# Layer 2 of a two-layer hybrid block: convolved tiles 2 to 5 and retention keys as three channel pairs of seven quarter products

## The reference, cut to what matters

```python
hx = modulate(rms_norm(x, norm1_g[layer]), mx[0], mx[1])
hc = modulate(rms_norm(ctx, norm1_g[layer]), mc[0], mc[1])
oc, ox = token_mixers(hc @ w_in[layer], hx @ w_in[layer], ...)
...
# gated delta net: q, k, v are convolved over the tokens of each half
qkv = jax.nn.silu(depthwise_conv_centred(qkv, conv_w))     # 5 taps per channel
# retention: latent queries and keys are turned by their position
ql, kl = apply_rope(ql, cos, sin), apply_rope(kl, cos, sin)
```

## Time and profile before

| | us |
|---|---|
| median of 3 runs | 2078.41 (2075.3 to 2080.1) |
| profiled execution, its own time | 2080.07 |
| its span (first to last instruction) | 2078.1 |
| PE busy | 1959.0 (94%) |
| DVE busy | 732.0 (35%) |
| ACT busy | 351.4 (17%) |
| POOL busy | 301.8 (15%) |

### The profile page before, as it was taken

The page is one execution under the profiler, slowest core; times in us unless marked ns, Lnnn a source line. Parts: engine busy times, 40 slices in busy tenths (PEclk is TensorE's granted clock), DMA queues, the critical chain, the costliest instruction groups (busy, mean ns, idle before and its releaser), DMA issues.

```text
span 2078.1 us, 53833 instructions
## 1 busy us (share of the span) xinstructions
PE 1959.0 (94%) x24244; PEld 1393.3 (67%) x24244; DVE 732.0 (35%) x1625; ACT 351.4 (17%) x845; POOL 301.8 (15%) x264
## 2 busy tenths in 40 slices
PE   6999987899999999999879899899999999999996
PEld 4885557578888888885677666466655666666664
DVE  5586547346553555356575500100101010000102
ACT  3005535121000000213552300000000000000001
POOL 0872524000000000096360000000000000000000
PEclk9999999999999999999989899899999999999998
DMA  9224562422213222321202999999999999999996
GB/s 348 83 82 162 203 243 84 163 82 80 83 61 102 82 82 76 128 82 41 82 3 104 350 366 378 403 408 342 328 404 401 403 401 398 401 405 399 408 392 235
DMA packets 181552, 481.99 MB, mean 232 GB/s; under 512 B 11738, under 2 KB 48458, under 8 KB 181194
## 3 DMA queue, kind: packets, MB, share of 16 engines
q1 hardware_dynamic: 177008, 473.99, 60.8%
q0 software_dynamic: 768, 2.62, 0.4%
q10 hardware_dynamic: 3546, 1.91, 0.3%
HBM read 476.39 MB, written 2.10 MB: 230 GB/s over the span
## 4 chain that ended last, share of the span: by engine, by line
PE 80%; DVE 6%; DMA 5%; POOL 3%; issue 3%; SPq 2%; ACT 1%; DVEq 0%; ACTq 0%; POOLq 0%
PE bank L785 77%; PE bank L788 3%; DMA ring<-in_moe_w_dram 3%; POOL ring L3562 2%; DMA ring<-in_w_in_dram 1%; POOL work L3564 1%; DMA ring<-in_ada_w_dram 1%; SPq L738 1%; DVE small L2695 1%; SPq L748 1%; ACT ring L1889 1%; DVE tmpB L2568 1%; DVE ring L2861 0%; POOL work L3560 0%; DVE ring L2523 0%
## 5 line engine op out<-in xcount | busy, mean ns | idle before, releaser
L785 PE MATMUL bank<-ring,hT 128*32 128x256 f32 (+1 forms) x10112 | 591.9, 380 | 6.0 <-DMA ring<-in_moe_w_dram 5.4
L785 PEld LDWEIGHTS bank<-ring,hT 128*32 128x32 f32 (+1 forms) x10112 | 357.5, 112 | 227.6 <-issue 19.6
L785 PE MATMUL bank<-ring 64*64 64x64 f32 (+5 forms) x4184 | 429.3, 292 | 30.0 <-issue 9.1
L785 PEld LDWEIGHTS bank<-ring 64*64 64x64 f32 (+3 forms) x4184 | 356.2, 157 | 89.6 <-issue 38.9
L785 PE MATMUL bank<-hT,ring 128*128 128x256 f32 (+1 forms) x1448 | 363.2, 407 | 6.3 <-DMA ring<-in_w_in_dram 2.6
L785 PEld LDWEIGHTS bank<-hT,ring 128*128 128x128 f32 x1448 | 278.2, 194 | 75.9 <-issue 35.5
L785 PE MATMUL bank<-ring,gates 128*32 128x256 f32 x4928 | 276.8, 382 | 9.2 <-DMA ring<-in_moe_w_dram 8.8
L785 PEld LDWEIGHTS bank<-ring,gates 128*32 128x32 f32 x4928 | 158.8, 111 | 119.4 <-DMA ring<-in_moe_w_dram 14.0
L1889 ACT ACTIVATE gates<-bank 128x256 f32<-128x256 f32 (+2 forms) x139 | 58.3, 465 | 902.1 <-PE bank L788 517.4
L3484 DVE TENSOR_TENSOR gates<-gates,bank 128x512 f32<-128x512 f32 (+1 forms) x42 | 22.5, 570 | 416.0 <-PE bank L785 416.0
L3641 POOL DMA_INDIRECT table<-token_rows,moe_index x8 | 7.4, 930 | 704.0 <-PE bank L788 593.7
(11 more groups left out here) (263 smaller groups left out, 1416.7 us busy)
## 6 DMA issues: line engine op xcount, KB each, us to landing
ring<-in_moe_w_dram SPq DMA_DIRECT2D x304, 1024.0 KB, 17.9
ring<-in_ada_w_dram SPq DMA_DIRECT2D x24, 2048.0 KB, 8.1
ring<-in_moe_w_dram SPq DMA_DIRECT2D x64, 512.0 KB, 11.2
ring<-in_ffn_w_dram SPq DMA_DIRECT2D x22, 1024.0 KB, 7.8
ring<-in_w_in_dram SPq DMA_DIRECT2D x10, 2048.0 KB, 8.6
ring<-in_w_out_dram SPq DMA_DIRECT2D x4, 2048.0 KB, 8.9
ring<-in_ffn_w_dram SPq DMA_DIRECT2D x4, 1536.0 KB, 6.7
ring<-in_ffn_w_dram SPq DMA_DIRECT2D x4, 1280.0 KB, 5.9
```

The lines of the kernel that those rows point to most:

```text
L785: return nc.tensor.matmul(o, w, x, start=start, stop=stop)
```

## The change

`IN_PAIRS` gets three entries, 9 to 11, which are pairs of layer 2: tiles 2 and 3, tiles 4 and 5, retention keys. `N_FIRST` is 9, the number of pairs of layer 1.

```diff
+                    ("gqk", 1), ("gvz", 0), ("rqk", 1)]
+        N_FIRST = 9
```

PE's order in `project_by_half`:

```diff
             def project_by_half():
 
+                (a11, a12), (_, a22) = in_blocks(9)
+                (b11, b12), _ = in_blocks(10)
                 pe.wait_ge(*weights(("gqk", 1)))
...
-                product(("gc", 1, 2))
-                channel(2, CONTEXT)
-                squares_sum(2, ("ss", 2), when("added_lat", (2, DT - 1)), (2, 3))
-                product(("gc", 1, 3))
-                channel(3, CONTEXT, range(4))
-                spread_root(("rstd", 2), when("inverse_root", 2), (2, 3))
-                channel(3, CONTEXT, range(4, DT))
-                pe.wait_ge(*weights(("gvz", 1)))
-                for c in (4, 5):
-                    product(("gc", 1, c))
-                    channel(c, CONTEXT)
-                for c in range(6):
-                    if c < 2:
-                        product(("gc", 1, c))
-                    channel(c, LATENTS)
+                pe.wait_ge(*when("mod_ctx", (2, 3)))
+                in_product("q1", 9, a11, xblock(0, 0))
+                pe.wait_ge(*when("mod_ctx", (2, DT - 1)))
+                in_product("q2", 9, a12, xblock(1, 0))
+                squares_sum(2, ("ss", 2), when("added_lat", (2, DT - 1)), (2, 3))
+                pe.wait_ge(*weights(("gvz", 1)))
+                in_product("q1", 10, b11, xblock(0, 0))
+                spread_root(("rstd", 2), when("inverse_root", 2), (2, 3))
+                in_product("q2", 10, b12, xblock(1, 0))
+                for c in range(2):
+                    o = product(("gc", 1, c))
+                    for k in range(DT):
+                        if c == 0:
                             pe.wait_ge(*when("mod", (2, k)))
...
+                in_sum_product("q5", 9, 1)
+                pe.wait_ge(*when("wcomb", ("in", 9, 4)))
+                in_product("q3", 9, in_w(9, 4), xblock(1, 1))
+                in_sum_product("q6", 9, 2)
+                in_sum_product("q7", 9, 3)
+                pe.wait_ge(*when("xcomb", ("in", 1, 4)))
+                in_product("q4", 9, a22, in_x(4))
+                fill_frees(("gqk", 1), ("q4", 9))
+                in_rest(10)
```

In `project`, behind the two latent tiles of retention queries:

```diff
-                        keys = [((name, l, c), c) for c in range(4)]
+                        keys = [((name, l, c), c) for c in range(2 if name == "rqk" else 4)]
...
+                    if name == "rqk":
+                        in_pair(11)
+                        key = ("q3", 11)
                     fill_frees((name, l), key)
```

ACT's `project`:

```diff
                 if l:
                     act.wait_ge(*when("pads", l))
-                for c in range(6 if l else 0):
+                    first_products(9, 11)
+                for c in range(2 if l else 0):
                     key = ("gc", l, c)
...
                     fn(acc2[:, c, :], acc2[:, c, :], ACT.Silu).then_inc(*mark("conv_silu", (l, c)))
+                    if (l, c) == (1, 2):
+                        first_products(11, 12)
```

DVE, ahead of `last_conv` and in `project`:

```diff
                     norm_after_ffn()
+                    in_weight_sums(9)
+                    in_x_sums(1, (1, 2, 3, 4))
+                    in_weight_sums(10)
+                    in_combine(9)
+                    in_combine(10)
                     last_conv()
...
-                for c in range(4 if l else 0):
-                    rope(("rqk", l, c), rqk[:, c, :], "rqk_ready", (l, c), needed(l) if c < 2 else 0)
+                if l:
+                    in_weight_sums(11)
+                for c in range(2 if l else 0):
+                    rope(("rqk", l, c), rqk[:, c, :], "rqk_ready", (l, c), CTX)
+                if l:
+                    in_pairs(11, 12)
```

More of the change, by code:

```diff
@@ L377, in in_blocks @@
             name, q = IN_PAIRS[i]
-            w = kslot(where[name, 0])
+            w = kslot(where[name, i // N_FIRST])
             return [[w[:, 4 * h:4 * h + 4, (2 * q + m) * P:(2 * q + m + 1) * P] for h in range(2)] for m in range(2)]
@@ L974, in first_in_pairs @@
                 in_sum_product("q7", 0, 3)
-                pe.wait_ge(*when("xcomb", ("in", 4)))
+                pe.wait_ge(*when("xcomb", ("in", 0, 4)))
                 in_product("q4", 0, in_blocks(0)[1][1], in_x(4))
@@ L983, in project_first @@
                 turn_vectors(1)
-                for i, (name, q) in enumerate(IN_PAIRS):
-                    if i < 2:
-                        continue
+                for i in range(2, N_FIRST):
+                    name, q = IN_PAIRS[i]
                     if name == "sq" and q == 0:
@@ L1014, in project @@
                     else:
-                        keys = [((name, l, c), c) for c in range(4)]
+                        keys = [((name, l, c), c) for c in range(2 if name == "rqk" else 4)]
                     for key, c in keys:
-                        keys_values = name == "kvab" or name == "rqk" and c >= 2
-                        by_channel(key, w, c, hT, 0 if keys_values else CTX)
+                        by_channel(key, w, c, hT, 0 if name == "kvab" else CTX)
                     if name == "kvab":
@@ new lines, in project_by_half @@
+                pe.wait_ge(*weights(("gvz", 1)))
[6 more added lines that the diff above has]
+                        if c == 0:
+                            pe.wait_ge(*when("mod", (2, k)))
+                        ins = mm(o[:, CTX:TOK], kslot(where["gqk", 1])[:, k, c * P:(c + 1) * P], hT[:, k, CTX:TOK],
+                                 k == 0, k == DT - 1)
+                    ins.then_inc(*filled(("gc", 1, c)))
@@ L2070, in project @@
                     act.wait_ge(*when("pads", l))
-                for c in range(6 if l else 0):
+                    first_products(9, 11)
+                for c in range(2 if l else 0):
                     key = ("gc", l, c)
                     act.wait_ge(*full(key))
-                    s0 = 1 if l and c < 2 else 0
-                    fn(cin[:, c, s0:2, 2:258], bank(key)[:, s0 * CTX:TOK].rearrange("p (s n) -> p s n", n=CTX),
-                       ACT.Copy).then_inc(*read(key))
+                    fn(cin[:, c, 1, 2:258], bank(key)[:, CTX:TOK], ACT.Copy).then_inc(*read(key))
                 if l == 0:
-                    first_products(2, len(IN_PAIRS))
+                    first_products(2, N_FIRST)
                     pair_done(act, 3)
@@ L2507, in in_weight_sums @@
                 name, _ = IN_PAIRS[i]
+                l = i // N_FIRST
                 (a11, a12), (a21, a22) = in_blocks(i)
@@ L2511, in in_weight_sums @@
                 if js[0] == 1:
-                    dve.wait_ge(*weights((name, 0)))
+                    dve.wait_ge(*weights((name, l)))
                     if i == 0:
@@ L2530, in in_x_sums @@
                     if j == 1:
-                        dve.wait_ge(*when("mod_ctx", (0, 3)))
-                        for k in range(DT):
+                        dve.wait_ge(*when("mod_ctx", (2 * l, 3)))
+                        for k in range(DT if l == 0 else 0):
                             dve.wait_ge(*when("mod_late", (0, k)))
+                        if l:
+                            dve.wait_ge(*when("mod", (2, 3)))
+                    if j == 2 and l:
+                        dve.wait_ge(*when("mod", (2, DT - 1)))
                     if j in (2, 4):
-                        dve.wait_ge(*when("xcomb", ("in", j // 2)))
+                        dve.wait_ge(*when("xcomb", ("in", l, j // 2)))
                     if j == 4:
-                        dve.wait_ge(*when("mod_ctx", (0, DT - 1)))
+                        dve.wait_ge(*when("mod_ctx", (2 * l, DT - 1)))
                     a, b = terms[j]
-                    v.tensor_tensor(in_x(j), a, b, ALU.subtract).then_inc(*mark("xcomb", ("in", j)))
+                    v.tensor_tensor(in_x(j), a, b, ALU.subtract).then_inc(*mark("xcomb", ("in", l, j)))
             def in_combine(i):
```

42 lines of the change are left out of this document (15 added, 27 removed).

## The result

The changed kernel takes 2087.35 us (median of 7 runs, 2085.32 to 2092.35), the kernel before 2080.1 on the same chip (7 runs, 2074.49 to 2081.47). The ratio is 1.0042, with a 95% interval of 1.0031 to 1.0053: slower by about 8.7 us (0.0042 x 2080), where 3.6 were forecast. The profiled execution took 2087.35 us for a span of 2085.4. A moment in a trace is compared after both have been set to the same zero, the row `bank<-table,hT 128x1 x4` with which PE closes the feed-forward: 859.16 before, 857.55 after, so 1.61 us is added to a time of after.

The account below looks back on a forecast made before the run. It took POOL's layer 2 convolutions to hold the critical chain to the first mask, with PE nearly full. The mask shift gave +4.8 or +2.2 us; the middle, +3.6 on 2078.4, made 2082.0 us, range 2075 to 2087.5.

Parts of the forecast that it names:

- POOL's first convolution: Layer 2 convolutions on POOL: the first starts near 878.6 instead of 885.6, 7.0 us early.
- The overlapped sums: DVE's input and weight sums beside POOL's convolution: 6.0 us alone, slowed 1.6 times to 9.7 us.
- PE's wait: In the projection, PE idles 6.7 us before q3(9) for a bank that DVE's first combine frees.
- Second wait: In the projection, PE waits 1.6 us before q6(10) for the bank freed by pair 10's first combine.
- Clock behind the first: PE's clock falls after its 6.7 us idle in the projection, losing 3.2 us, bounds 0 and 3.4.
- First mask: First window scores masked 7.2 us after PE's projection ends, at 964.8, 4.8 us later than before.
- rival (a): Likeliest case: bank wait in the projection and slow clock behind it, +2.2 to +4.8 us; chance 0.50.
- rival (b): The bank wait comes but the clock doesn't fall: 3.2 less, -1.0 to +1.6 us, near 2078.7; chance 0.22.
- rival (c): DVE's sums run at lone speed, PE waits 3.0 us, no clock fall: faster, 2073.6 to 2076.2; chance 0.13.
- I carry a shift to the end one to one: Everything behind the first mask depends on that stage, so its shift reaches the kernel's end unchanged.
- the middle of +4.8 and +2.2: End shift taken as +3.6 us, between the window's clock falling as before (+4.8) and its 2.7 loss vanishing (+2.2).
- Rival (d): POOL slows DVE 1.9 times throughout, second wait drops the clock again: +7 to +10 us, 2086 to 2088; chance 0.10.

Follow-up runs that it names:

- experiment 3: Changed kernel with the product ahead of PE's first wait issued four times, keeping PE busy: 1.0031 of the kernel before, +6.4 us.
- experiment 6: Changed kernel with POOL's first layer-2 convolution held until DVE's last weight sum of pair 10: 1.0041 of the kernel before, +8.5 us.
- Experiment 1: Kernel before with only the bank counter moved on by 15 behind the projection of layer 2: 1.0027 of the kernel before, +5.6 us.
- experiment 2: Changed kernel with the bank counter moved on by 105, so later banks are those of before: 1.0022 of the kernel before, +4.6 us.
- experiment 5: Changed kernel with first combines of pairs 9 and 10 ahead of later sums, bank counter plus 105: 0.9991 of the kernel before, -1.9 us.
- experiment 8: Changed kernel with retention keys plain, only tiles 2 to 5 as pairs, combines late, bank counter plus 110: 1.0015 of the kernel before, +3.1 us.
- experiment 11: Changed kernel with retention keys plain, early combines, ACT's gate exponentials moved ahead, bank counter plus 110: 0.9965 of the kernel before, -7.3 us.

## Why the prediction was wrong

**Up to the first mask every step held.** The working that was open to doubt came out close to its number:
- POOL's first convolution: 878.6 forecast, 877.18 + 1.61 = 878.8. Its last ends at 947.86 + 1.61 = 949.5, where 949 was forecast.
- The overlapped sums: 9.7 us forecast, with a factor of 1.6; 9.2 from 878.12 to 887.31, a factor of 1.5. It was a mean of unlike parts: the second group of weight sums has 1.96 (5.13 / 2.62), while of the three input sums that overlap only two were slowed. The first combine was forecast at 889.7 and is out at 887.31 + 0.41 + 1.61 = 889.3.
- PE's wait: 6.7 forecast, 6.13. Second wait: 1.6, 1.66. Clock behind the first: 0.50, with 3.2 us reckoned and 3.0 gained at the mask by experiment 3.
- End of projection 957.6, and 956.03 + 1.61 = 957.6. First mask 964.8, and 965.0.

So the wait of rival (a) is real, rival (b) (a clock that stays) fell by the trace, and rival (c) needed sums that run at their lone speed; experiment 6 gave just that, with the wait of 3.0 us that (c) names (2.90) and no fall of the clock, and then POOL, held back for it, stood on the chain again.

**The step that failed is the last: "I carry a shift to the end one to one".** A shift of 5.0 us at the mask became 9.2 at the experts, as no term stood for the bank counter behind the mask. The sum went wrong in two places.
1. The shift was taken as the middle of +4.8 and +2.2: the clock fell in the window all the same, behind 1.22 + 2.09 us, and the 16 records took 6.65 us, more than the 6.11 before. The middle of two branches is a time that neither gives; the branch was +4.8, worth 1.2 us on the sum. (By its own terms the lower branch is 4.8 - 2.7 = 2.1 and the middle 3.5, not 3.6.)
2. No term stood for the bank counter. The stage behind the mask was taken to be the same instructions in the same places, but the places are counted from the products made before. Experiment 1 gives that term +5.6 us by itself, experiment 2 takes 4.1 off the change. With it the sum would have been 4.8 plus 4.1 to 5.6, or +8.9 to +10.4, and +8.7 was measured.

The prediction named the sign that it would fail by: a shift at the first expert product that differs from that at the first mask by over 2 us. It differs by 4.1. Rival (d) had the size (+7 to +10), but by another mechanism: its second fall of the clock behind the 1.66 us wait did not come (32 records in 7.14 us behind it are full speed). The measured 2087.35 us lies just under the upper end of the stated range, 2087.5; that is luck, as the range goes that high for (d) alone.

**What stays open.** The keys' pair alone costs 4.6 us by its time and 2.2 by its trace; experiment 6 has +5.4 at the start of the experts and +8.5 in the time; experiment 5 has -4.6 and -1.9. These three differ by 2.4 to 3.1 us. In the other nine kernels with an edit, the start of the experts and the time agree within 2 us (+9.2 and +8.7 for the change; then in the order of the experiments +6.0 and +5.6, +5.8 and +4.6, +5.8 and +6.4, +2.7 and +4.2, +2.7 and +3.1, -7.5 and -5.6, -4.6 and -4.8, -8.2 and -7.3). A trace shows one execution, and a part of the spread lies outside the stage: over the thirteen traces the zero stands at 856.47 to 859.88, and from the start of the experts to the end of the span it is 906.0 to 908.7 us. So one trace settles a mechanism and not the last 3 us of a time.

## What to carry to other kernels

- A counter that deals out buffers carries a change to places that it doesn't touch. Where instructions are added or taken away ahead of a counter, work out their number modulo every period in use; a shift of the counter alone is a cheap test, in both directions.
- Work that frees another engine's buffer comes ahead of work that only prepares what comes later: the first combine in front of the sums took away two waits, and PE ended its projection 11.3 us earlier than in the changed kernel (87.15 instead of 98.48 us behind the zero).
- Before an engine's work is shortened, look at what stands in program order behind a wait that it doesn't need. Here that was one block on ACT, worth 5.6 us.

## What was not expected of the hardware

- The clock did not fall behind 2.90 us of idle time in one piece (8 records in 1.97 us, experiment 6), and fell behind 1.22 and 2.09 us with 3.2 us between their ends (16 records in 6.65 us). Behind 1.76 us the same 16 records took 5.38 in experiment 8, behind 1.75 us they took 3.69 in experiment 11, at a granted clock of 1.00. So the length of one idle time doesn't tell by itself.
- The Trainium skill (TensorE: Matmul & The Clock Gate, Part 1: The HAM clock gate) has the array fall to 1.2 GHz when idle and come back under sustained work. The trace agrees behind 6.13 us (0.50); behind idle times of 1 to 3 us the rows above go both ways.
- DVE and POOL slow each other. The convolution's first two operations took 2.62 and 2.70 us beside the sums (experiment 5), where the earlier trace rows has 1.57. Of the input sums of 128 x 1024 beside POOL, those of two tiles (`ring<-hT,ring`) took 1.53 and 1.62 us, and the one between them, which reads two parts of one tile, 1.21, as alone.
- The rule of the Trainium skill that the prediction weighed (GPSIMD Engine Reference, 1. Specifications) names contention for VectorE instructions with two SBUF inputs, and not which engine loses by it. The sum between has two such inputs and was not slowed; POOL's operation that began just ahead of it, at 879.43, took 2.70 us. So the trace agrees that the engines contend, and not that each such VectorE instruction is slower for it.
